# Block 2's modulation summed on VectorE beside block 1's value tiles, and GpSimd's work in pieces of 256

## The reference, cut to what matters

```
mod = c @ w_mod + b_mod                     # block 2: silu(c_2) @ w_ada_2 + b_ada_2; 1024 -> 6 * 1024
sh1, sc1, gt1, sh2, sc2, gt2 = split(mod, 6)
h = modulate(rmsnorm(x, g), sh1, sc1) ...   # mixer, x = x + gt1 * out
h2 = modulate(rmsnorm(x, g2), sh2, sc2)
q  = h2 @ w_query                           # 8 heads x 2 halves x 128
s1, s2 = top 16 of q against the sub-keys;  cand = s1[:, None] + s2[None, :];  top 16 of 256
a  = gelu(h2 @ expert_u[chosen]) * softmax(gates)
x  = x + gt2 * (a @ expert_v[chosen])
```

## Time and profile before

| What | Value |
|---|---|
| Median of 3 runs | 2326.63 us (2326.26 to 2330.02) |
| The profiled execution's own time | 2326.31 us |
| Its span, first to last instruction | 2324.5 us |
| TensorE's mean granted clock | 0.984 |
| TensorE busy (matmuls) | 2216.7 us, 95% |
| VectorE busy | 1546.4 us, 67% |
| ScalarE busy | 1197.9 us, 52% |
| GpSimd busy | 350.5 us, 15% |
| HBM read | 403.99 MB, 174 GB/s over the span |

### The profile page before, as it was taken

How to read it: one execution, slowest core, us unless ns; L and a number is a source line. 1 busy time by engine, 2 the same in 40 slices (tenths; PEclk the granted TensorE clock), 3 DMA queues, 4 the chain that set the end, 5 groups by cost and what they waited for, 6 DMA issues and landing times.

```text
span 2324.5 us, 39500 instructions
## 1 busy us (share of the span) xinstructions
PE 2216.7 (95%) x15524; PEld 2021.1 (87%) x15524; DVE 1546.4 (67%) x2924; ACT 1197.9 (52%) x2141; POOL 350.5 (15%) x231
## 2 busy tenths in 40 slices
PE   7999899999999999999988998999999999999998
PEld 5988899999999887877777888999999998888886
DVE  2354669898999764544554545498889998555555
ACT  3455444445777554444444453444447776555453
POOL 1322000102222334334300000001011221000000
PEclk9999999999999999999999999999999999999999
DMA  8664455555333567777642443555554334566663
GB/s 321 208 209 162 159 187 175 180 180 165 120 126 128 160 222 252 257 254 249 223 141 90 129 136 100 172 170 169 180 172 140 124 128 142 183 192 193 196 192 127
DMA packets 110551, 407.61 MB, mean 175 GB/s; under 512 B 11552, under 2 KB 11936, under 8 KB 110112
## 3 DMA queue, kind: packets, MB, share of 16 engines
q1 hardware_dynamic: 98928, 361.81, 47.8%
q10 hardware_dynamic: 11440, 43.28, 4.9%
HBM read 403.99 MB, written 1.05 MB: 174 GB/s over the span
## 4 chain that ended last, share of the span: by engine, by line
PE 77%; DVE 13%; ACT 4%; issue 4%; DMA 1%; SPq 0%; POOL 0%; DVEq 0%; ACTq 0%
PE PB L431 22%; PE PB L433 21%; PE PB L432 21%; DVE WL L1457 5%; PE PB L752 4%; ACT WH L1031 3%; PE PB L496 2%; DVE OH L1815 1%; DMA AR<-in_wm 1%; DVE AR L1732 1%; DVE AR L1720 1%; PE PB L1001 1%; PE PB L727 1%; PE PB L475 1%; DVE OH L1812 1%
## 5 line engine op out<-in xcount | busy, mean ns | idle before, releaser
L1457 DVE TENSOR_TENSOR WL<-RING,WH 128x1024 fp32r<-128x1024 f32 x564 | 732.3, 1301 | 475.3 <-ACT WH L1031 473.7
L1031 ACT ACTIVATE WH<-RING 128x1024 fp32r<-128x1024 f32 x651 | 686.3, 1055 | 441.5 <-PE PB L433 437.9
L431 PE MATMUL PB<-HH,WH 128*128 128x256 f32 x2848 | 827.0, 290 | 25.5 <-DVE WL L1457 15.6
L433 PE MATMUL PB<-HH,WL 128*128 128x256 f32 x2848 | 810.9, 285 | 0.0
L432 PE MATMUL PB<-HL,WH 128*128 128x256 f32 x2848 | 810.6, 285 | 0.0
L431 PEld LDWEIGHTS PB<-HH,WH 128*128 128x128 f32 x2848 | 550.7, 193 | 34.2 <-issue 26.5
L432 PEld LDWEIGHTS PB<-HL,WH 128*128 128x128 f32 x2848 | 550.4, 193 | 0.2
L433 PEld LDWEIGHTS PB<-HH,WL 128*128 128x128 f32 x2848 | 549.5, 193 | 0.0
L431 PE MATMUL PB<-WH,HH 128*128 128x512 f32 (+2 forms) x1344 | 497.8, 370 | 23.0 <-POOL WL L2071 5.4
L432 PE MATMUL PB<-WL,HH 128*128 128x512 f32 (+2 forms) x1344 | 492.8, 367 | 0.0
L433 PE MATMUL PB<-WH,HL 128*128 128x512 f32 (+2 forms) x1344 | 492.7, 367 | 0.0
(11 more groups left out here) (211 smaller groups left out, 1541.5 us busy)
## 6 DMA issues: line engine op xcount, KB each, us to landing
RING<-in_u SPq DMA_DIRECT2D x256, 512.0 KB, 3.3
RING<-in_v SPq DMA_DIRECT2D x256, 512.0 KB, 4.3
RING<-in_win SPq DMA_DIRECT2D x90, 512.0 KB, 3.5
AR<-in_wm ACTq DMA_DIRECT2D x40, 1024.0 KB, 6.1
RING<-in_wq SPq DMA_DIRECT2D x32, 512.0 KB, 3.3
AR<-in_wm SPq DMA_DIRECT2D x8, 1024.0 KB, 15.5
RING<-in_wout SPq DMA_DIRECT2D x16, 512.0 KB, 3.4
RING<-in_sk SPq DMA_DIRECT2D x8, 512.0 KB, 3.4
```

The costliest lines, as they stand in the source:

```text
L431: e.matmul(o, ah, bh, start=start, stop=False)
L433: return e.matmul(o, al, bh, start=False, stop=stop)
L1031: e.activation(hi(t), raw(("w", t), words(t)), ACT.Copy).then_inc(s_hi, 1)
L1457: e.tensor_tensor(lo(t), raw(("w", t), words(t)), hi(t).bitcast(F32), ALU.subtract).then_inc(s_lo, 1)
```

## The change

Block 2's chunks go to VectorE. `chunk_step` (new) takes chunk g = 24 + i over four iterations n of block 1's V stretch, from n = 22 + 4i on, two instructions per iteration, one ahead of `fill` and one behind it: the first is `MR = w_0 * c_0`, the seven others `MR = w_t * c_t + MR`, with the condition as a column scalar. TensorE keeps `columns`, five tiles after the chunk's first. ScalarE issues chunk g + 2 when `s_mdv` says that chunk g is summed. `COND` is no longer written for block 2, and its bias is added at n = 121. `on_pool` loses the odd V tiles. GpSimd's low parts are cut into four instructions of 256 elements, and the candidate sums and EQ products into eight, one per head; the signal comes with the last.

```diff
-IN_V = {30 + 4 * i: 24 + i for i in range(24)}
+V_FIRST = 22
+IN_V = {V_FIRST + 4 * i: 24 + i for i in range(24)}
 def on_pool(n):
-    return n == 0 or n % 2 == 1 and (3 <= n < 48 or W_V + 2 <= n < W2_Q)
+    return n == 0 or n % 2 == 1 and 3 <= n < 48
...
# TensorE, columns(g)
-                e.wait_ge(s_mev, g + 1)
+                if g < 24:
+                    e.wait_ge(s_mev, g + 1)
+                else:
+                    e.wait_ge(s_mdv, g - 23)
+                if g == 24:
+                    e.wait_ge(s_mod, 7)
...
# TensorE, peer, after value tile n
-                    if blk == 0 and n in IN_V:
-                        mod_step(IN_V[n])
+                    if blk == 0 and n - 5 in IN_V:
+                        columns(IN_V[n - 5])
...
-                if blk == 0:
-                    columns(47)
...
# ScalarE, peer, iteration n
-                    if blk == 0 and n == 26:
-                        e.wait_ge(s_al, NK * blk + 28)
+                    if blk == 0 and n == V_FIRST - 4:
+                        e.wait_ge(s_al, 12 + 8)
                         chunk_in(24)
+                    if blk == 0 and n == V_FIRST + 4:
+                        e.wait_ge(s_al, 12 + 16)
                         chunk_in(25)
-                    if blk == 0 and n in IN_V:
-                        mod_step(IN_V[n])
+                    if blk == 0 and n - 4 in IN_V and IN_V[n - 4] < 46:
+                        e.wait_ge(s_mdv, IN_V[n - 4] - 23)
+                        chunk_in(IN_V[n - 4] + 2)
...
# VectorE
+            def chunk_step(n, half):
+                i, t = (n - V_FIRST) // 4, 2 * ((n - V_FIRST) % 4) + half
+                if not 0 <= i < 24:
+                    return
+                g = 24 + i
+                w, rows, c = chunk(g)[:, t // 4, t % 4, :], MR[:, g % 2, :], SM[:, C_C2 + t:C_C2 + t + 1]
+                if t == 0:
+                    e.wait_ge(s_silu, 1)
+                    e.wait_ge(s_mcol, g - 1)
+                    e.wait_ge(*chunk_landed(g))
+                    chunk_sum[0] = own.mark(e.tensor_scalar(rows, w, c, None, ALU.mult))
+                    return
+                own.done(chunk_sum[0])
+                r = e.scalar_tensor_tensor(out=rows, in0=w, scalar=c, in1=rows, op0=ALU.mult, op1=ALU.add)
+                if t < 7:
+                    chunk_sum[0] = own.mark(r)
+                else:
+                    r.then_inc(s_mdv, 1)
...
                     stage(n + 2)
+                    if blk == 0:
+                        chunk_step(n, 0)
                     fill(n_v + n)
-                    if blk == 0 and n == 16:
-                        e.wait_ge(s_silu, 1)
-                        conditions(C_C2)
+                    if blk == 0:
+                        chunk_step(n, 1)
+                        if n == V_FIRST + 4 * 24 + 3:
+                            e.wait_ge(s_mcol, 48)
+                            add_bias(48, C_B2, 0, 48)
...
# GpSimd, low_parts
-                        e.tensor_tensor(lo(t), raw(("w", t), words(t)), hi(t).bitcast(F32), ALU.subtract).then_inc(s_lop, 1)
+                        for o in range(0, words(t), 256):
+                            r = e.tensor_tensor(lo(t)[:, o:o + 256], raw(("w", t), words(t))[:, o:o + 256],
+                                                hi(t)[:, o:o + 256].bitcast(F32), ALU.subtract)
+                        r.then_inc(s_lop, 1)
...
# GpSimd, peer
-                    e.tensor_tensor(CA[:, :, :].rearrange("p h (i j) -> p h i j", i=16),
-                                    vv[:, :, 0, :].unsqueeze(3).to_broadcast([128, 8, 16, 16]),
-                                    vv[:, :, 1, :].unsqueeze(2).to_broadcast([128, 8, 16, 16]), ALU.add).then_inc(s_cand, 1)
+                    for h in range(8):
+                        r = e.tensor_tensor(CA[:, h, :].rearrange("p (i j) -> p i j", i=16),
+                                            vv[:, h, 0, :].unsqueeze(2).to_broadcast([128, 16, 16]),
+                                            vv[:, h, 1, :].unsqueeze(1).to_broadcast([128, 16, 16]), ALU.add)
+                    r.then_inc(s_cand, 1)
...
-                        e.tensor_tensor(eq, eq, ff[:, :, s, :].unsqueeze(2).to_broadcast([128, 8, 16, 16]),
-                                        ALU.mult).then_inc(s_em, 1)
+                        for h in range(8):
+                            r = e.tensor_tensor(eq[:, h], eq[:, h], ff[:, h, s, :].unsqueeze(1).to_broadcast([128, 16, 16]),
+                                                ALU.mult)
+                        r.then_inc(s_em, 1)
```

More of the change, by code:

```diff
@@ L210, in two_block_kernel @@
         s_pn = sem("s_pn")
+        s_mdv = sem("s_mdv")
         s_silu, s_cond, s_mpe, s_mev, s_mcol, s_mod = sem("s_silu"), sem("s_cond"), sem("s_mpe"), sem("s_mev"), sem("s_mcol"), sem("s_mod")
@@ L490, in mod_chunk @@
                         e.wait_ge(s_up, 3)
-                    if g in (8, 12, 24):
-                        e.wait_ge(s_mod, {8: 4, 12: 5, 24: 7}[g])
-                e.wait_ge(s_cond, 2 if MODS[g][0] else 1)
+                    if g in (8, 12):
+                        e.wait_ge(s_mod, {8: 4, 12: 5}[g])
+                e.wait_ge(s_cond, 1)
                 for u in range(2):
@@ L500, in mod_step @@
             def mod_step(g):
-                if g not in (N_START, 12, 24):
+                if g not in (N_START, 12):
                     columns(g - 1)
@@ L1103, in mod_step @@
                 chunk_out(g)
-                if g + 2 not in (20, 21, 24, 25, 48, 49):
+                if g + 2 not in (20, 21):
                     chunk_in(g + 2)
@@ L1792, in choose @@
                     e.tensor_copy(GIT[:, s, :], PB[4 + s][:, 0:256]).then_inc(s_git, 1)
+            chunk_sum = [0]
+            def chunk_step(n, half):
[16 more added lines that the diff above has]
+                    r.then_inc(s_mdv, 1)
             def peer(blk, n_q, n_u, n_v, gate):
@@ L1886, in peer @@
                 fill(n_v + NK - NW)
-                if blk == 0:
-                    e.wait_ge(s_mcol, 48)
-                    add_bias(48, C_B2, 0, 48)
                 e.wait_ge(s_fg[blk], 16)
```

## The result

The changed kernel takes 2307.32 us, the median of four runs (2299.15 to 2310.01), against 2328.32 us for the kernel before on the same chip: a ratio of 0.9902 [0.9873, 0.9931]. It is faster, by 20 to 21 us where 32 were forecast, and its time lies 2.3 us above the predicted range. Its profiled execution took 2306.42 us of its own, with a span of 2304.6.

A forecast was written before the change was run, and what follows sets the result against it. TensorE's own instruction list was taken to bound the value stretches, with waits for VectorE's low parts in the key stretches. Terms -24.0 - 9.5 + 1.2 = -32.3 from 2326.3 us gave 2294, range 2285 to 2305.

The forecast's parts named there:

- case A: Whole kernel: the main forecast, all parts as worked out, 2291 to 2298 us; chance 0.50.
- Part 1: Block 1's value stretch: chunk sums leave TensorE, 1.00 us saved in each of 24 steps, 24.0 us.
- Part 2: Block 1's value stretch: VectorE's added sums and odd tiles' low parts stay hidden, priced at 0.
- Rival E: Block 1's value stretch: VectorE becomes the bound, from 0.69 us an instruction; 2353 us at 1.0 us; chance 0.04.
- D: Value stretch: TensorE gains only about half, waiting 0.5 us a period, 2306 us; chance 0.11.
- Part 3: Waits and transfers, including chunks landing before they are needed, cost nothing: 0.
- Part 4: Key stretches: pieces let VectorE's low parts in, 9.5 us saved, bounds 0 and 15.1.
- B: Key stretches: GpSimd is not held up by VectorE, all 15.1 us of waits go, 2288 us; chance 0.17.
- C: Key stretches gain nothing: VectorE not let in, or the late reduction gives the stalls back; 2304 us; chance 0.16.
- Part 5: Start: GpSimd's low parts in pieces end later at two tiles TensorE waits for, +1.2 us in all.

The follow-up runs named there:

- chunk 25 in time: Changed kernel with the sums starting three value tiles later, chunk 25's transfer still issued at tile 26: 2301.93 us, ratio 0.9889 against the kernel before.
- the doubled sums: Changed kernel with seven more VectorE sum instructions per chunk, their results unused: 2306.97 us in a single run.
- the kernel with the long instructions whole: Changed kernel with candidate sums and EQ products each one instruction of 2048 again, low parts still in pieces: 2311.91 us, ratio 0.9923.
- Low parts whole: Changed kernel with GpSimd's low parts of tiles 0 to 47 each one instruction of 1024 again: 2295.9 us, ratio 0.9854 against the kernel before.
- tile 47 alone: Changed kernel with only tile 47's low part given to VectorE, GpSimd's other low parts still in pieces: 2299.81 us, ratio 0.9874.
- no low part on GpSimd: Changed kernel with no low parts on GpSimd at all, candidate sums and EQ products still in pieces: 2297.84 us, ratio 0.9862.

## Why the prediction was wrong

The sign and case A's mechanism held; the time missed by 2306.4 - 2294 = 12.4 us in the profiled execution. By its steps:

- **Part 1 (-24.0), right.** The sums leave TensorE's list and the restart behind the columns costs less than I kept for it: a step costs 0.50 in place of 0.57 us. 25.7 by the period, 1.7 better, and in the kernels with chunk 25 in time 25.7 or 27.2 arrive.
- **Part 2 (0), right.** VectorE at 40.83 of 50 lies in the forecast 38 to 43, the new instruction at 0.478 in 0.42 to 0.55. It occupies about 0.40, not 0.34. That the work is hidden is shown by the doubled sums, which are not. Rival E's mechanism exists: by the doubled sums it begins at an estimated 0.74 us an instruction, where 0.69 was worked out, and this change stays far under it. D, a wait in each period, did not happen.
- **Part 3 (0), wrong for one chunk: +2.9.** The failed step is "A chunk is needed four tiles (11.4 us) after its issue, and landed in 6.1 us". It holds for the chunks that are issued in `chunk_in(IN_V[n - 4] + 2)`. Chunks 24 and 25 have lines of their own in the diff, and chunk 25's issue and first use both stand at n = 26. VectorE waited 6.46 us, about a transfer's usual time (6.1); the lead was nought.
- **Part 4 (-9.5), right in mechanism, 1.5 too much.** With the candidate sums and EQ products whole again the two stretches are 8.0 us longer. VectorE and GpSimd exclude one another as worked out: the product ended at 424.21 + 8.51 = 432.7, 8.5 us after its start, with 5.0 + 3.4 = 8.4 us worked out for the two in turn. Four waits of 1.4 us are left at the low part behind the reduction, two in each block, as forecast, but to the tenth by luck: 417.74 + 8.4 is 426.1 and not the 426.5 that the prediction goes on with, and from 426.1 the stall comes out at 1.0. What the sum did not have is the last reduction, which is late for the transposes as well, 2.5 us in place of 0.2 in each block. Against that, some gain stands in no wait of the list: against the kernel with the long instructions whole, block 1's waits fall by 2.4 us (7.4 + 0.2 to 2.9 + 2.5, and 0.2 for `in_sk`) and its stretch by 3.7. The other 1.3 are, by estimate, the restarts: there are eight such waits in that kernel and three in the changed one, and 5 x 0.24 = 1.2 us. The other 1.6 of the 9.6 in the table is block 2's key stretch of the kernel before, which was granted 0.98 from 1460 to 1560 us; the kernel with the candidate sums and EQ products whole had 1.00 there and took 455.1 in place of 456.7. B (GpSimd not held up) and C (VectorE not let in) both fell.
- **Part 5 (+1.2), wrong: +8.2.** This is the step that decided the miss. "One VectorE instruction (0.69 or 1.14) may come between": at tile 47 two low parts came between, and the pieces took 4.75 us where I allowed 2.6 + 1.14 = 3.7. "The other odd tiles up to 47 have slack for it": two of them now have a wait, 0.94 and 0.87 us at 66.93 and 81.97, where the kernel before has none. TensorE's waits for GpSimd rise by 5.2 us in all, of which tile 47 is 2.8. And no term stood for what comes with a wait: 5.2 us of waiting go with 8.2 of time. Of the other 3.0, 2.0 are the slow matmuls behind tile 47 and some 0.5 the restarts of two more waits; the rest is no more than the scatter of the start. Low parts whole returned 6.9, tile 47 alone 4.8, and no low part on GpSimd 8.7.
- **Clock, no term: +2.7.** Middle +2.7 (granted 0.95 in place of 0.96) and value 2 +1.6 (0.92 in place of 1.00 in its first 21 us), less the 1.6 of key 2. No edit is shown to cause it: the middle scatters by 7.4 us from profile to profile, and the changed kernel's profile lies on the long side of that by chance, as far as the runs show.

Sum of the miss: 7.0 (part 5) + 2.9 (part 3) + 1.5 (part 4) + 2.7 (clock) - 1.7 (part 1) = 12.4.

I used one law, the exclusion of VectorE and GpSimd, in full in part 4, where pieces let VectorE in and this helps, and in part 5, where the piecewise side is the one that TensorE waits for, only for a single instruction at two tiles. The Trainium skill ("SBUF — State Buffer", section "Who interferes with whom") calls the port pair that the two share an exclusive lock, in which the order of issue decides who blocks. The traces agree on both sides: a low part of 1.23 us lasted 4.54 beside a whole candidate sum and 1.47 beside the pieces; GpSimd's four pieces, with two low parts of VectorE between, lasted 4.75.

## What to carry to other kernels

Cutting a long instruction that shares something with another engine does not make the sharing cheaper, it changes who is late: cut where the other engine is the urgent one, and leave whole, or move away, the work that the bounding engine itself waits for. Where work moves in a pipeline, check the first and the second item by their own lines; the steady state's lead says nothing about them. A wait of TensorE costs more than its row says, here 0.24 us at a restart and 2.0 more where the clock fell behind a wait of 4.35 us, so a forecast that adds such waits needs a second term, from a row where the clock fell.

## What the runs showed of the hardware that I had not expected

GpSimd's recorded durations do vary once there is something to vary with. The groups of its pieces, by line (count, busy us, mean ns):

```profile
L2103 POOL TENSOR_TENSOR WL<-RING,WH 128x256 fp32r<-128x256 f32 x96 | 74.1, 802 | 173.8 <-ACT WH L1036 173.8
...
L2124 POOL TENSOR_TENSOR AR<-AR 128x256 f32<-128x256 f32 x64 | 68.1, 1101 | 196.6 <-DVE AR L1781 196.6
L2116 POOL TENSOR_TENSOR AR<-AR 128x256 f32<-128x256 f32 x32 | 30.7, 993 | 969.6 <-DVE AR L1733 969.6
```

The medians are 0.737, 0.750 and 0.644 us, the longest 2.79, 1.73 and 1.61: a piece that finds VectorE at work is held up by it. Undisturbed, a piece costs more than its share of the whole instruction, by the medians 0.737 against 2.39 / 4 = 0.60, and 0.644 against 3.68 / 8 = 0.46; some 0.14 to 0.18 us for each more instruction.

The same instructions at the same place in the program differ by up to 7.4 us from profile to profile (the middle stretch, 343.7 to 351.1). This is a third of what the whole change brought, and the granted clock over the stretch goes with it, 0.97 to 0.93.
